# The first pair's mixers: half of the values' convolution ahead of retention's heads, the delta rule's output norm started during the first of two gates

## The reference, cut to what matters

```python
u = rmsnorm(h, g_norm)
rq, rk, rv, rg, gqkv, gz, ga, gb, mg_ret, mg_gdn = split(u @ w_in)
# retention: 4 heads, q and k rotated
o = retention(rotary(rq), rotary(rk), rv)            # per head: scores, output
o = (o - mean(o)) * rsqrt(var(o) + EPS) * ret_gn
y_ret = (o * silu(rg)) @ w_br_ret
# gated delta rule: 8 heads, in two chunks here of 128 tokens
gq, gk, gv = split(silu(causal_conv(gqkv, conv_w)))  # 4 taps along the tokens
o = gated_delta_rule(l2norm(gq), l2norm(gk), gv, g, beta)
o = o * rsqrt(mean(o * o) + EPS) * gdn_gn
y_gdn = (o * silu(gz)) @ w_br_gdn
h = h + (sigmoid(mg_ret) * y_ret + sigmoid(mg_gdn) * y_gdn) @ w_out
```

## Time and profile before

| what | value |
|---|---|
| median of three runs | 2468.59 us |
| profiled execution | 2469.0 us, span 2467.2 us |
| mean granted TensorE clock | 0.964 |
| PE busy | 2291.2 us, 93% |
| PE weight load busy | 2119.9 us, 86% |
| DVE busy | 1577.4 us, 64% |
| ACT busy | 1377.3 us, 56% |
| HBM traffic | 160 GB/s over the span |

### The profile page before, as it was taken

One profiled execution on the slowest core, in us unless ns is written; L12 is line 12 of the kernel. 1 busy time (PEld: TensorE's weight loads), 2 busy tenths in 40 slices (PEclk: granted clock), 3 DMA queues, 4 the chain that ended last, 5 costly groups with the idle time before them and its releaser, 6 DMA issues.

```text
span 2467.2 us, 38778 instructions
## 1 busy us (share of the span) xinstructions
PE 2291.2 (93%) x16290; PEld 2119.9 (86%) x16290; DVE 1577.4 (64%) x2235; ACT 1377.3 (56%) x1910; POOL 19.9 (1%) x14
## 2 busy tenths in 40 slices
PE   7989999999999899998999999999669999877999
PEld 6979998999999799997888888788559998756999
DVE  4666555666575665463888888867646665754765
ACT  5754546544566554554777777766444444654443
POOL 0000000000000000000000000000000000000000
PEclk9999999999999899997999999999879999988999
DMA  6531234555454213341888888954114564412453
GB/s 230 155 110 52 95 104 145 171 175 186 156 166 158 92 52 103 112 158 70 315 297 300 302 307 307 313 186 137 57 35 145 180 197 146 140 35 77 163 188 137
DMA packets 111205, 398.12 MB, mean 161 GB/s; under 512 B 12336, under 2 KB 12336, under 8 KB 110768
## 3 DMA queue, kind: packets, MB, share of 16 engines
q1 hardware_dynamic: 111024, 395.58, 48.1%
HBM read 394.48 MB, written 1.05 MB: 160 GB/s over the span
## 4 chain that ended last, share of the span: by engine, by line
PE 66%; DVE 16%; ACT 11%; DMA 6%; issue 2%; SPq 0%; DVEq 0%; ACTq 0%
PE ps L413 65%; DVE wlo L2008 7%; DMA raw<-stream 5%; ACT whi L1234 4%; ACT arena L1244 3%; DVE arena L2008 2%; DVE arena L2016 1%; DVE scr L2008 1%; ACT scr L1244 1%; ACT arena_r L1244 1%; DVE h L2008 1%; DMA CO<-const 1%; ACT L1244 1%; ACT rst L1244 1%; DVE scr L2016 0%
## 5 line engine op out<-in xcount | busy, mean ns | idle before, releaser
L2008 DVE TENSOR_TENSOR wlo<-raw,whi 128x1024 fp32r<-128x1024 f32 (+1 forms) x762 | 901.6, 1197 | 552.0 <-ACT whi L1234 542.2
L1234 ACT ACTIVATE whi<-raw 128x1024 fp32r<-128x1024 f32 (+1 forms) x762 | 781.3, 1035 | 347.3 <-PE ps L413 268.0
L413 PE MATMUL ps<-uh,whi 128*128 128x256 f32 (+1 forms) x2240 | 654.3, 292 | 13.9 <-ACT scr L1244 6.2
L413 PE MATMUL ps<-ul,whi 128*128 128x256 f32 (+1 forms) x2240 | 635.4, 284 | 0.0
L413 PE MATMUL ps<-uh,wlo 128*128 128x256 f32 (+1 forms) x2240 | 635.0, 284 | 0.0
L413 PE MATMUL ps<-arena_r,whi 128*128 128x256 f32 x2720 | 491.3, 283 | 19.7 <-DVE arena_r L2008 12.3
L413 PEld LDWEIGHTS ps<-uh,whi 128*128 128x128 f32 (+1 forms) x2240 | 429.7, 192 | 25.9 <-issue 17.4
L413 PEld LDWEIGHTS ps<-arena_r,whi 128*128 128x128 f32 x2720 | 420.0, 190 | 24.5 <-DVE arena_r L2008 13.4
L413 PEld LDWEIGHTS ps<-ul,whi 128*128 128x128 f32 (+1 forms) x2240 | 429.9, 192 | 6.0 <-issue 5.2
L413 PEld LDWEIGHTS ps<-uh,wlo 128*128 128x128 f32 (+1 forms) x2240 | 429.4, 192 | 0.0
L413 PE MATMUL ps<-arena_r,wlo 128*128 128x256 f32 x1360 | 381.9, 281 | 0.0
(11 more groups left out here) (163 smaller groups left out, 1902.5 us busy)
## 6 DMA issues: line engine op xcount, KB each, us to landing
raw<-stream SPq DMA_DIRECT2D x694, 512.0 KB, 4.1
raw<-stream SPq DMA_DIRECT2D x64, 384.0 KB, 4.2
CO<-const SPq DMA_DIRECT2D x1, 2305.0 KB, 13.2
h<-xT SPq DMA_DIRECT2D x1, 1024.0 KB, 5.8
raw<-stream SPq DMA_DIRECT2D x4, 256.0 KB, 2.6
out<-h SPq DMA_DIRECT2D x4, 256.0 KB, 2.2
arena<-pT SPq DMA_DIRECT2D x2, 256.0 KB, 3.9
SM<-small SPq DMA_DIRECT2D x1, 464.0 KB, 3.2
```

The lines of the kernel that those rows point to most:

```text
L413: return self.e.matmul(o, l, r, start=start, stop=stop, skip_group_check=True)
L1234: self.e.activation(M.whi[:, b:b + n], M.raw[:, a:a + n], ACT.Copy).then_inc(K.sem("weight_hi"), 1)
L2008: return self.e.tensor_tensor(o, a, b, op)
```

## The change

`side` now runs the first four pieces of the values' convolution before the heads, in rounds 16 to 19 and with banks of the common ring, and the other four beside the heads (rounds 20 to 35, pieces in 21, 23, 25 and 27), still in bank 5. The last rotation follows the first of these pieces. On ACT the silu of the first two tiles comes with the fourth step, that of the next two just before the heads. `g1` and `g2` are in rounds 36 to 51, `gz` in 52 to 59 and `gg` in 60 to 67. `finish` runs beside both gates, after five empty steps.

```diff
+def idle(n):
+    for _ in range(n):
+        yield
@@ Tensor.side
-        vconv = self.proj_T(self.ring((5,)), s, ("vconv", l), "w_in", l, 5120, 1024)
-        next(vconv)
-        yield
-        self.rotate(work, s, l, 6)
+        for n, _ in enumerate(self.proj_T(work, s, ("vconv", l, 0), "w_in", l, 5120, 512)):
+            yield
+            if n == 0:
+                self.rotate(work, s, l, 6)
+        vconv = self.proj_T(self.ring((5,)), s, ("vconv", l, 4), "w_in", l, 5632, 512)
         yield from beside(self.heads(self.ring((6, 7)), s, l), vconv, 2)
...
-        yield from self.proj_T(work, s, ("gz", l), "w_in", l, 6144, 1024)
-        yield from beside(self.proj_T(work, s, ("gg", l), "w_in", l, 8208, 1024), self.finish(work, s, l), 1)
+        gates = chain(self.proj_T(work, s, ("gz", l), "w_in", l, 6144, 1024),
+                      self.proj_T(work, s, ("gg", l), "w_in", l, 8208, 1024))
+        yield from beside(gates, chain(idle(5), self.finish(work, s, l)), 1)
@@ Scalar.side
-        vconv = self.vconv(s, l)
-        next(vconv)
-        yield
-        yield from beside(self.heads(s, l), vconv, 2)
+        yield from self.vconv(s, l, 0)
+        self.vsilu(s, l, 2)
+        yield from beside(self.heads(s, l), self.vconv(s, l, 4), 2)
...
-        yield from self.straight(s, ("gz", l), ACT.Silu, M.A["gz"])
-        yield from beside(self.straight(s, ("gg", l), ACT.Sigmoid, M.A["rg"]), self.finish(self.thread_scr, s, l), 1)
-
-    def vconv(self, s, l):
-        for tt in range(8):
+        gates = chain(self.straight(s, ("gz", l), ACT.Silu, M.A["gz"]), self.straight(s, ("gg", l), ACT.Sigmoid, M.A["rg"]))
+        yield from beside(gates, chain(idle(5), self.finish(self.thread_scr, s, l)), 1)
+
+    def vconv(self, s, l, at):
+        for tt in range(4):
             self.ahead()
             if tt % 2:
-                self.conv_tap(s, l, ("vconv", l), tt - 1, 16)
-                if tt > 2:
-                    self.vsilu(s, l, tt - 3)
-            yield
-        self.vsilu(s, l, 6)
+                self.conv_tap(s, l, ("vconv", l, at), tt - 1, 16 + at)
+            if tt == 3:
+                self.vsilu(s, l, at)
+            yield
+        if at:
+            self.vsilu(s, l, 6)
@@ Vector.side
-        vconv = self.vconv(s, l)
-        next(vconv)
-        yield
-        self.rotate(s, l, 6)
-        yield from beside(self.heads(s, l), vconv, 2)
+        for n, _ in enumerate(self.vconv(s, l, 0)):
+            yield
+            if n == 0:
+                self.rotate(s, l, 6)
+        yield from beside(self.heads(s, l), self.vconv(s, l, 4), 2)
...
-        for _ in range(8):
-            self.ahead()
-            yield
-        yield from beside(self.aheads(8), self.finish(s, l), 1)
+        yield from beside(self.aheads(16), chain(idle(5), self.finish(s, l)), 1)
```

More of the change, by code:

```diff
@@ L1588, in side @@
                 yield
-        yield from self.straight(s, ("gz", l), ACT.Silu, M.A["gz"])
-        yield from beside(self.straight(s, ("gg", l), ACT.Sigmoid, M.A["rg"]), self.finish(self.thread_scr, s, l), 1)
-    def vconv(self, s, l):
-        for tt in range(8):
+        gates = chain(self.straight(s, ("gz", l), ACT.Silu, M.A["gz"]), self.straight(s, ("gg", l), ACT.Sigmoid, M.A["rg"]))
+        yield from beside(gates, chain(idle(5), self.finish(self.thread_scr, s, l)), 1)
+    def vconv(self, s, l, at):
+        for tt in range(4):
             self.ahead()
             if tt % 2:
-                self.conv_tap(s, l, ("vconv", l), tt - 1, 16)
-                if tt > 2:
-                    self.vsilu(s, l, tt - 3)
+                self.conv_tap(s, l, ("vconv", l, at), tt - 1, 16 + at)
+            if tt == 3:
+                self.vsilu(s, l, at)
             yield
-        self.vsilu(s, l, 6)
+        if at:
+            self.vsilu(s, l, 6)
     def vsilu(self, s, l, t):
-        self.silu(s, ("vconv", l), t, self.M.A["qkv"][:, (16 + t) * T:(18 + t) * T], ("vsil", l, t))
+        self.silu(s, ("vconv", l, t // 4 * 4), t % 4, self.M.A["qkv"][:, (16 + t) * T:(18 + t) * T], ("vsil", l, t))
     def ret_values(self, l, g):
@@ L2398, in aheads, with vconv @@
             yield
-    def vconv(self, s, l):
-        for tt in range(8):
+    def vconv(self, s, l, at):
+        for tt in range(4):
             self.ahead()
             if tt % 2:
-                self.conv_taps(s, l, ("vconv", l), tt - 1, 16)
+                self.conv_taps(s, l, ("vconv", l, at), tt - 1, 16 + at)
             yield
```

## The result

The changed kernel takes 2463.28 us (median of 20 runs, 2458.21 to 2469.6), the kernel before 2468.15 beside it (20 runs). The ratio is 0.9984, 95% interval 0.9976 to 0.9992: some 4 us faster by the ratio (4.9 between the medians), where 20 were forecast. The time lies 2.3 above the range's upper end. The profiled execution has a span of 2459.2 us.

The account below looks back on a forecast made before the run. PE was taken as the bound, busy 93% of the span, so only its waits and low clock could yield. Gains of 10.6 (layer 0) and 9.6 (layer 1), together 20.2, off 2468.6 gave 2448 us; range 2438 to 2461.

Parts of the forecast that it names:

- part two: Output norm beside both gates: its steps keep their delta-rule steps; branch wait 3.87 goes, low clock too (2.6 and 1.6).
- the two bank waits: Gates, rounds 58 and 64: norm's sums share the ring of three banks; 0.75 each, 1.5 lost per layer.
- The rival for the tail: Output norm beside the gates: ACT's table loads slow `finish`, the branch still waits 3.87 at low clock; 2460, chance 0.09.
- Part one: Half the values' convolution ahead of the heads: V0's bank wait goes, delta rule starts 2.5 earlier; 5.6 gained per layer.
- The levels: First chunk, rounds 20 to 35, with fewer convolution pieces: old waits of 2.2 go, new 2.1 come; net 0.
- The third and fourth rivals: Rounds 28 to 35: clock falls, 2475, chance 0.06; or the chain through ACT and DVE binds, 2463, chance 0.07.
- the fourth rival: Rounds 28 to 35 bound by the ACT and DVE chain, a wait over 1.2 in each; 2463, chance 0.07.
- The branch: Branch projection after the gates: wait of 3.87 goes whole, and the first piece takes 3 us at full clock.
- the three signs: Forecast wrong if rounds 28 to 35 wait over 5 us, clock there under 0.9, or pre-delta-rule wait gone or grown.
- the first two rivals: Head gains little, 2455 or 2460, chance 0.10; tail's branch wait and low clock stay, 2460, chance 0.09.
- the levels' bound: Rounds 28 to 35: a wait of 0.75 in each of eight rounds, less 2.2; 3.8 lost per layer.

Follow-up runs that it names:

- five, order and banks mended: Changed kernel, five empty steps, with the norm's step ahead of the gate's activation on ACT and the norm's sums in banks 0 to 4: 2453.81 us, 0.9938.
- the kernel with the norm's own banks: Changed kernel, five empty steps, with the norm's sums in banks 0 to 4 instead of the shared ring: 2460.76 us, 0.9976.
- the kernel with the new order: Changed kernel, five empty steps, with the norm's step between a piece's split and the gate's activation on ACT: 2466.98 us, 0.9997.
- part two alone with five steps: Kernel before, with only the output norm run beside both gates after five empty steps, convolution unmoved: 2467.98 us, 0.9995.

## Why the prediction was wrong

**The step that failed** is the one on part two: "So its steps stay with the same steps of the delta rule" is true, and I took it for the whole answer. What matters is which step of the gates they meet. The gates began three rounds later and `finish` at the same round, so the norm moved by an odd number of steps against the activations in ACT's queue. I had counted the bank takes of that stretch in order, and the table loads, but not what each ACT instruction waits for while the norm stands behind it. The runs showed in its place a wait of 3.76 and 3.77 us before the second norm sum, with the low clock after it. With the two bank waits it cost 12.4 us, where 3.0 had been charged: six empty steps, with nothing else changed, give 2450.84; with five, order and banks mended, 2453.81. The rival for the tail put ACT's table loads in doubt, but expected the delay at the branch, where it wasn't: three pieces of cover there hide it, and it came out at the norm's own second sum, which is PE's.

**The wait on POOL**, 1.0 per layer, was missed in the same way: `gz` was moved by three rounds past the delta rule's exp on ACT.

**Part one**: right in mechanism. V0 has no wait; the delta rule's first matmul comes 3.0 us earlier against the last rotations (forecast 2.5); the wait ahead of it is 4.68 (4.6). Counted as the forecast counts it, with two pieces more and 2.85 of head 0 less, the gain up to round 20 is 6.1 us in layer 0 and 5.9 in layer 1, where I had 5.6.

**The levels** were the term of this part that was mis-sized. From round 20 to round 39 PE takes 97.52 us before and 87.36 after in layer 0, 96.84 and 87.16 in layer 1. With five pieces fewer and head 0's 2.85 more, that is 1.7 and 2.2 us lost, where I had put nothing, inside the bounds given. It isn't the waits, which are 0.6 shorter than before, nor the clock, 0.96 to 0.97 on the mean in both: the same matmuls keep PE busy some 2.5 us longer, and why stays open.

**Rounds 20 to 35**: the waits are 1.6 (forecast 2.1), and once it had recovered from the stop before the delta rule the clock held. The window from round 22 through round 36 of the kernel after, some 30 us of it (219.8 to 249.5) without a piece:

```profile
190.50:252.50 62.00, 59.91 (x463) 56.80 (x462) 36.60 (x74) 27.47 (x46) 0.00 (x0) 1.00 0.12 35
```

The third and fourth rivals fall with it. So does the rule of the Trainium skill ("TensorE: Matmul & The Clock Gate", section "A second HAM failure mode: psum-queue depth-cycling") for this case: short idles between matmul groups, 0.15 to 0.72 us here, did not make the clock swing. That the fourth rival had named the measured time, 2463, is chance: its waits are not there.

**The branch**: its wait of 3.87 is gone, and its first piece runs from 404.19 at a clock of 1.00. **The bank waits**: 0.78 twice, as forecast; with six empty steps they are not there, since sum matmuls lie in between again.

The chances were too sure as well. All my rivals for the tail were about whether the wait goes; none about a new one elsewhere in the chain that was moved. None of the three signs that I had named for the forecast being wrong came true, as all of them were about the first chunk and the wait ahead of it. And the range's upper end, 2461, took the first two rivals and the levels' bound one at a time; together they pass 2470.

## What to carry to other kernels

When work of one thread is shifted against another on engines that run in order, check the alignment on every engine, not only the one that waits: ask of each shifted instruction what now stands ahead of it in its queue, and what that is waiting for. Where both threads have a rhythm of two steps, an odd shift can cost the whole gain and the even one next to it nothing, so run both. And a wait can have two causes that hide each other (here ACT's order and a shared ring of banks): that an edit changes little doesn't clear its cause until the other is gone too.

## What was not expected of the hardware

The price of a stop lies partly in the clock that follows. After the wait of 4.7 us before the delta rule the granted clock was 0.50 for some 9 us, and after the wait of 3.76 in the gates it was 0.50 for some 3, where the sum's matmuls took 3.29 us instead of 1.88. The length of a stop alone does not give this price. After the 4.77 before the second sum in the kernel with the norm's own banks the clock was low for some 3 us too; after the waits of 2.25 in the kernel with the new order it fell, and after the wait of 2.19 in part two alone with five steps it stayed at 1.00 (384 to 390 us). In the two executions of the kernel before and after, the time at the low clock around the first model's two mixers came to 37.6 and 27.2 us by windows of 5 us. At half speed that difference is worth some 5 us; the waits fell by 4.0 in both layers together.
